# Rotary units of a two-block kernel: the halves of the head channels changed over by ScalarE's eviction copies, in place of a TensorE product with a permutation matrix

## The reference, cut to what matters

```
def rotary(t):                       # t: (B,H,L,d), d = 128
    ang = jnp.arange(l)[:, None] * inv_freq[None, :]
    cos, sin = jnp.cos(ang), jnp.sin(ang)
    t1, t2 = tf[..., : d // 2], tf[..., d // 2:]
    return jnp.concatenate([t1 * cos - t2 * sin, t1 * sin + t2 * cos], axis=-1)

def retention_branch(q_in, k_in, v_in, g_in, onorm_g):
    q = rotary(to_heads(q_in, RET_HEADS))
    k = rotary(to_heads(k_in, RET_HEADS)) * (dk ** -0.5)
    ...
    o = chunked_scalar_decay(q, k, to_heads(v_in, RET_HEADS), log_a)
```

## Time and profile before

| | us |
|---|---|
| median of 3 runs (lowest, highest) | 3839.66 (3838.66, 3841.17) |
| the profiled execution, device time | 3837.98 |
| its span, first to last instruction | 3835.6 |
| PE busy in the span | 3659.7 (95%) |
| DVE busy | 1949.5 (51%) |
| ACT busy | 1532.6 (40%) |

### The profile page before, as it was taken

The page is one execution under the profiler, slowest core; times in us unless marked ns, Lnnn a source line. Parts: engine busy times, 40 slices in busy tenths (PEclk is TensorE's granted clock), DMA queues, the critical chain, the costliest instruction groups (busy, mean ns, idle before and its releaser), DMA issues.

```text
span 3835.6 us, 45492 instructions
## 1 busy us (share of the span) xinstructions
PE 3659.7 (95%) x18866; PEld 2904.6 (76%) x18866; DVE 1949.5 (51%) x2542; ACT 1532.6 (40%) x1770; POOL 71.2 (2%) x54
## 2 busy tenths in 40 slices
PE   7999999979999997999999999999999999999998
PEld 5877666766666665777888888787777888888787
DVE  4454444365555554464556653444564556653434
ACT  4332112255555543432445632333432456633333
POOL 0000000000000001000000000000000000000000
PEclk9999999999999998999999999999999999999999
DMA  5101443279999984100111011333010111011332
GB/s 192 44 25 50 155 146 119 98 289 369 372 370 369 367 330 165 39 34 33 50 39 50 34 56 45 143 125 122 34 44 24 50 39 50 34 56 45 120 127 99
DMA packets 92306, 474.88 MB, mean 124 GB/s; under 512 B 10160, under 2 KB 10800, under 8 KB 54208
## 3 DMA queue, kind: packets, MB, share of 16 engines
q1 hardware_dynamic: 77360, 417.37, 29.5%
q0 software_dynamic: 8976, 33.56, 2.3%
q10 hardware_dynamic: 5760, 20.97, 1.3%
HBM read 414.72 MB, written 57.15 MB: 123 GB/s over the span
## 4 chain that ended last, share of the span: by engine, by line
PE 52%; DVE 4%; ACT 4%; issue 2%; DMA 0%; DVEq 0%; ACTq 0%; POOLq 0%
PE ps L136 13%; PE ps L138 13%; PE ps L137 13%; PE ps L1737 3%; PE ps L1582 1%; PE ps L1562 1%; PE ps L1556 1%; PE ps L1983 1%; PE ps L316 1%; PE ps L1525 1%; PE ps L1721 1%; DVE WA L3585 1%; PE ps L3514 1%; PE ps L3481 0%; PE ps L3502 0%
## 5 line engine op out<-in xcount | busy, mean ns | idle before, releaser
L136 PE MATMUL ps<-HH,WS 128*128 128x512 f32 (+1 forms) x2608 | 1050.0, 403 | 21.1 <-DVE WS L1339 10.5
L138 PE MATMUL ps<-HH,WS 128*128 128x512 f32 (+1 forms) x2608 | 1022.4, 392 | 0.0
L137 PE MATMUL ps<-HL,WS 128*128 128x512 f32 (+1 forms) x1968 | 771.9, 392 | 0.0
L136 PEld LDWEIGHTS ps<-HH,WS 128*128 128x128 f32 (+1 forms) x2608 | 493.3, 189 | 144.1 <-issue 24.5
L138 PEld LDWEIGHTS ps<-HH,WS 128*128 128x128 f32 (+1 forms) x2608 | 491.6, 188 | 107.2
L1402 ACT ACTIVATE WA<-ps 128x512 f32<-128x512 f32 x240 | 143.2, 598 | 901.9 <-PE ps L138 808.0
L137 PEld LDWEIGHTS ps<-HL,WS 128*128 128x128 f32 (+1 forms) x1968 | 372.7, 189 | 79.1 <-issue 5.1
L1339 DVE TENSOR_TENSOR WS<-RAW,WS 128x1024 fp32r<-128x1024 f32 (+1 forms) x153 | 200.6, 1312 | 197.9 <-ACT WS L1334 197.9
L136 PE MATMUL ps<-WS,HH 128*128 128x256 f32 x896 | 263.2, 294 | 12.3 <-DVE HL L2215 12.2
L137 PE MATMUL ps<-WS,HH 128*128 128x256 f32 x896 | 256.1, 286 | 0.0
L138 PE MATMUL ps<-WS,HL 128*128 128x256 f32 x896 | 255.9, 286 | 0.0
(11 more groups left out here) (400 smaller groups left out, 5353.2 us busy)
## 6 DMA issues: line engine op xcount, KB each, us to landing
WR<-in_weu SPq DMA_DIRECT2D x37, 1024.0 KB, 6.2
WR<-in_weg SPq DMA_DIRECT2D x35, 1024.0 KB, 7.9
WR<-in_wed SPq DMA_DIRECT2D x34, 1024.0 KB, 9.1
RAW<-in_wo SPq DMA_DIRECT2D x32, 1024.0 KB, 4.8
H<-in_wed SPq DMA_DIRECT2D x26, 1024.0 KB, 9.3
WA<-in_wada SPq DMA_DIRECT2D x48, 512.0 KB, 4.6
H<-in_weg SPq DMA_DIRECT2D x23, 1024.0 KB, 8.1
H<-in_weu SPq DMA_DIRECT2D x21, 1024.0 KB, 6.2
```

Of the source, the lines that this page charges most:

```text
L136: t.matmul(o, l[0], r[0], start=st, stop=False)
L137: t.matmul(o, l[0], r[1], start=False, stop=False)
L138: return t.matmul(o, l[1], r[0], start=False, stop=sp)
```

## The change

The copy of `u` stays. Behind each of its halves ACT reads the same PSUM bank twice more, partitions 64 to 127 to partitions 0 to 63 of `rs` and the other way round, and then signals `swapped`; the bank comes free by `swapped`, not `copied`. The two matmuls with `PERM` for each tile go, with their banks, the matrix, its load and its place among the inputs. DVE multiplies `rs` by `sin'` in place, in one instruction of 1024 columns for the two of 512. In the plan `rs` is taken ahead of the projection and ahead of `ro`.

```
@@ plan_prep_r
             for z in range(2):
-                yield from plan_copied(U, f"u{z}", "u", U, z)
+                wa.take("u", U, z)
+                wa.take("rs", U, z)
+                yield from plan_project(U, f"u{z}", lambda i: ("swapped", U, z, i))
                 wa.take("ro", U, z)
-                wa.take("rs", U, z)
-                for i in range(2):
-                    brief("perm", U, z, i, end=("rsin", U, z, i))
-                wa.give(("u", U, z), ("rcos", U, z), ("perm_mm", U, z, 1))
+                wa.give(("u", U, z), ("rcos", U, z))
                 wa.give(("rs", U, z), ("rot", U, z))
@@ tensor_prep_r
                 yield from tensor_project(t, U, f"u{z}")
-                if U == 8:
-                    t.wait_ge(*at("small_in", "perm"))
-                for i in range(2):
-                    free(t, banks, "perm", U, z, i)
-                    t.wait_ge(*at("copied", "u", U, z, 1))
-                    t.matmul(ps("perm", U, z, i), PERM, half(tl("u", U, z), i), start=True, stop=True).then_inc(
-                        *up("perm_mm", U, z, i))
@@ scalar_prep_r
             for z in range(2):
-                yield from scalar_project(a, U, f"u{z}", ("u", U, z))
+                for i, _ in enumerate(scalar_project(a, U, f"u{z}", ("u", U, z))):
+                    b, s = ps("pj", *number(U, f"u{z}"), i), half(tl("rs", U, z), i)
+                    if i == 0:
+                        free(a, wa, "rs", U, z)
+                    a.activation(s[0:64, :], b[64:128, :], ACT.Copy)
+                    a.activation(s[64:128, :], b[0:64, :], ACT.Copy).then_inc(*up("swapped", U, z, i))
+                    yield
@@ vector_prep_r
                 v.tensor_tensor(o, tl("u", U, z), rc(U)[0], ALU.mult).then_inc(*up("rcos", U, z))
-                free(v, wa, "rs", U, z)
-                for i in range(2):
-                    v.wait_ge(*at("perm_mm", U, z, i))
-                    v.tensor_tensor(half(s, i), ps("perm", U, z, i), half(rc(U)[1], i), ALU.mult).then_inc(*up("rsin", U, z, i))
-                v.wait_ge(*at("rsin", U, z, 1))
+                v.wait_ge(*at("swapped", U, z, 1))
+                v.tensor_tensor(s, s, rc(U)[1], ALU.mult).then_inc(*up("rsin", U, z))
+                v.wait_ge(*at("rsin", U, z))
@@ tensor_prep_g
-            t.wait_ge(*at("small_in", "perm"))
+            t.wait_ge(*at("small_in", "gk"))
@@ sync_program
-            s.dma_start(PERM, d["perm"]).then_inc(*up("small_in", "perm", by=16))
```

More of the change, by code:

```diff
@@ L187, in build @@
         GK = sb("GK", [16, 512])
-        PERM = sb("PM_", [128, 128])[:, :]
         bank_aps = [ctx.enter_context(nc.psum_tensor(f"ps{i}", [128, 512], F32))[:, :] for i in range(8)]
@@ L4294, in constants @@
         rot[3][:, 512 + h * 128:512 + (h + 1) * 128] = np.exp(lg * (127 - t)) * 128 ** -0.5
-    perm = (s == (t + 64) % 128).astype(np.float32)
-    return ct, rm, lm.reshape(128, 448), rot, perm
+    return ct, rm, lm.reshape(128, 448), rot
 def kernel(**inputs):
@@ L4314, in heads @@
         return fm(np.concatenate([w[:, o + h * 128:o + (h + 1) * 128] for o in offs], axis=1))
-    ct, rm, lm, rot, perm = constants()
-    a = {"ct": ct, "rm": rm, "lm": lm, "rot": rot, "perm": perm}
+    ct, rm, lm, rot = constants()
+    a = {"ct": ct, "rm": rm, "lm": lm, "rot": rot}
     a["xT"] = f["x"][0].T
```

## The result

| | before | changed |
|---|---|---|
| median of the runs (lowest, highest), us | 3840.41 (3838.66, 3841.26), 4 runs | 3806.49 (3803.92, 3812.72), 4 runs |
| ratio, 95% interval | | 0.9915 (0.9897 to 0.9932) |
| profiled execution / its span | 3837.98 / 3835.6 | 3803.92 / 3802.1 |

The gain of the medians is 33.9 us; 36.2 were forecast, and the median lies 3.0 us above the forecast of 3803.5. 0.75 us of these 3.0 is the kernel before, whose median is 3840.41 us with four runs where the forecast started from 3839.66. The first question is whether the places gave what was worked out; the second is where a difference of a few us can come from.

The account below looks back on a forecast made before the run. PE was taken to bound the rotary stage; 4 x 1.72 + 4 x 1.85 + 8 x 2.74 = 36.2 us off the 3839.66 us median gave 3803.5 us, own range 3800 to 3807 (0.82), wider range 3799 to 3811.

Parts of the forecast that it names:

- every term of the sum: Gains at 16 rotary places: 4 x 1.72, 4 x 1.85 and 8 x 2.74 us, together 36.2 us.
- What bounds: Layer 0's rotary stage: PE sets the time, busy 211.94 of 215.05 us; ACT has about 150 us free.
- The price by place: PE's start-to-start distances with and without the permutation: 1.72 us behind a core step, 1.85 behind the turn, 2.74 behind a pass.
- The wait goes with the product: At eight L138 places, PE's 0.78 us idle for the eviction goes, since the next pass does not read `u`.
- rival 1: At the eight L138 places as much waiting returns for something else: 6.2 us, so 3809.7 us; chance 0.08.
- ACT's copies: 64 copies behind the evictions, 0.50 us each, 1.00 a pair, 32 us of ACT in all, hidden from PE.
- the upper bound: Price of one ACT copy with no overlap: 0.60 us.
- DVE, banks, load, cover: DVE gains a quarter us a place off the path; later banks and the removed load count nothing; weight's cover stays 2.10 us.
- That L2005 hides the copies: On DVE, copies end at about 2324.6 and L2005 at 2324.94, so the wait for `swapped` is hidden.
- Rival 4: At four L1502 places dear copies hold PE at L1525; each us of a pair above 4.56 costs 4; chance 0.02.
- the same 4.56 us of cover: Time from the turned tile's eviction (L1509) ending at 2309.36 to PE needing it for L1525 at 2313.92.
- rival 2: Half-level clock stretches fall elsewhere, 1.6 us each, three more or fewer: 3798.7 to 3808.3 us; chance 0.05.

Follow-up runs that it names:

- extra3: Changed kernel with three more ACT copies of 64 partitions ahead of each pair: 3800.42 us; second time 3805.92 us, beside 3807.13 for the changed kernel.

## Why the prediction was right

The mechanism was right, and so was every term of the sum. That the median came as near as 3.0 us to the forecast is in part luck, since its four runs lie between 3803.9 and 3812.7 us.

- **What bounds.** PE did. Its waits in the stages went to none, and every us that left its queue left the stage.
- **The price by place.** It was worked out with places of the same trace that lacked the product, and each kind gave what was said, 36.2 us together. From durations it would have gone wrong: `L1983 x4` lasts 1.96 us in the earlier trace rows, costs 1.72 where it is moved away, and 2.74 with its wait.
- **The wait goes with the product.** It did. Put back alone it costs 8.1 us; rival 1 had 6.2, the idle shown, and an idle costs more than its own length.
- **ACT's copies.** Hidden, as said. The price was mis-sized: 1.34 us a pair for 1.00 (the upper bound was 1.20, the estimate by the page 1.04), because the starts lose their overlap, the one behind the pair too. It is not on the path, so nothing in the sum moved. ACT was to be near 79 us busy in the stage; it was 80.35 us (2245.68 to 2442.00).
- **DVE, banks, load, cover.** L2004 took 1.23 us, and no wait of PE for a bank or `w_lo` appeared, nor one of ACT for `rs`. That L2005 hides the copies was not quite so: DVE waits 0.02 to 0.03 us for `swapped`, as the pair lasts longer than the 1.00 us taken. The cover of DVE's result, up to the scores, holds this and also the 1.82 us of `extra3`.
- **Rival 4.** Its place was right, its slope too small: the same 4.56 us of cover did hold three more copies (3.2 us with them) and not eight more (6.4 us), but beyond it a us costs more than 4, since ACT's queue carries its delay on and the waits bring stretches at the half clock.
- **The 2.3 us that are missing.** No cause of its own is shown for them: they lie within the interval of the ratio, and the other medians of the changed kernel gained 36.7 and 34.0 us. What can be shown is where the two profiled executions differ from the sum. The stages give -36.38, the part ahead +4.04, between and behind -1.13, which make -33.47 for the span; 0.6 us less around it give the 34.1 between the two executions. Of the part ahead 3.4 us go with the half level of the clock, which is the effect of rival 2, on top of the forecast and not in place of it. Rival 2 allowed 4.8 us either way, at 1.6 us a stretch; over the traces the part ahead alone moved from -7.4 to +7.1. So an edit worth under some 5 us needs the stage's own length, not the kernel's time.

The Trainium skill ("ScalarE: Activation LUTs", What ACT_TABLE_LOAD costs) takes 93 ns off where two activations stand back to back. The trace about agrees where the first partitions stay (0.50 and 0.47 us between starts for a duration of 0.60), and does not where they change (0.59 to 0.62 us for a duration of 0.58 to 0.60).

## What to carry to other kernels

Where one engine is busy without a gap, price a removed instruction by the distance between the starts of its neighbours, with it and at a twin place without it in the same trace: the duration alone misses both overlap and wait. Moving work to an engine that is half idle is free only while every result still comes before it is asked for. Measure that cover at the tightest consumer, and count the backlog of all that follows, not one piece. When the times of two kernels differ by less than their runs spread, compare the stretch that the edit touches between fixed instructions: here it repeated to 0.01 us while the total moved by several.

## What was not expected of the hardware

- A copy by ACT overlaps the end of the one ahead only with the same first partition to read from and to write to: 0.49 to 0.50 and 0.47 us between starts against 0.59 to 0.62 (512 columns), 0.26 to 0.29 against 0.38 to 0.39 (256 columns). Crossing partitions costs nothing more: 594 and 590 ns for the crossing copies of the changed kernel, 579 and 593 ns for the straight ones.
- An idle of 0.69 us on PE in front of a projection cost 0.96 us from start to start, at the full granted clock.
- The 14 profiled executions put 105.8 to 126.3 us at the half level into the same 2.26 ms of the program, and the same idle of 2.12 us was followed by the half level in one and by the full level in another.
